# Scores of the first attention over all 128 rows of TensorE, with the queries doubled by on-chip transfers

## What is computed

```python
def diff_attention_mixer(h, hc, w_in, w_out, lam_p, subln_g, lam_init, cos, sin, with_ctx_out):
    # h: 256 tokens, hc: 256 context tokens; 8 heads, each with two query and two key vectors of 64 features
    q, k, v, z = project(h)
    qc, kc, vc, zc = project(hc)
    q, k = apply_rope(q, cos, sin), apply_rope(k, cos, sin)
    k_all, v_all = concat([k, kc]), concat([v, vc])
    def diff(qq, kk, vv, gate):
        o1 = sweep_attention(qq[..., 0, :], kk[..., 0, :], vv)     # softmax(q k / 8) v
        o2 = sweep_attention(qq[..., 1, :], kk[..., 1, :], vv)
        o = rms_norm(o1 - lam * o2, subln_g) * (1.0 - lam_init)
        return (o.reshape(B, L, 1024) * silu(gate)) @ w_out
    y = diff(q, k_all, v_all, z)          # tokens look at 512 keys
    yc = diff(qc, kc, vc, zc)             # the context looks at its own 256 keys
```

## Time and profile before

| | |
|---|---|
| median of 3 runs | 783.16 us |
| profiled execution, first to last instruction | 781.2 us |
| PE busy | 771.8 us, 99% |
| VectorE (DVE) busy | 550.9 us, 71% |
| ScalarE (ACT) busy | 395.9 us, 51% |
| chunks 1 to 5 of in0 | about 62 to 179.5 us |
| first attention, iterations 0 to 31 | 179.5 to 285 us |
| DMA in 193 to 278 us | 1% of the 16 engines, 1 GB/s |
| granted TensorE clock | 1.00 in every slice |

### The profile page before, as it was taken

How to read it: one execution, slowest core, us unless ns; L and a number is a source line. 1 busy time by engine, 2 the same in 40 slices (tenths; PEclk the granted TensorE clock), 3 DMA queues, 4 the chain that set the end, 5 groups by cost and what they waited for, 6 DMA issues and landing times.

```text
span 781.2 us, 10963 instructions
## 1 busy us (share of the span) xinstructions
PE 771.8 (99%) x4001; PEld 616.0 (79%) x4001; DVE 550.9 (71%) x988; ACT 395.9 (51%) x752; POOL 41.6 (5%) x54
## 2 busy tenths in 40 slices
PE   8999999999999999999999999999999999999998
PEld 5668777887777888867788888788788888888886
DVE  3356999797768868599767666998968554565553
ACT  4462323327788765475656656725444443443441
POOL 0020000000001010112100002200010000000000
PEclk9999999999999999999999999999999999999999
DMA  9995663344000075339222045963225745665621
GB/s 324 356 367 194 216 215 121 112 146 163 1 1 1 1 277 207 101 121 351 74 92 100 5 154 171 377 223 108 87 67 196 264 167 162 196 212 185 200 69 55
DMA packets 75576, 125.76 MB, mean 161 GB/s; under 512 B 2842, under 2 KB 36972, under 8 KB 75396
## 3 DMA queue, kind: packets, MB, share of 16 engines
q1 hardware_dynamic: 74576, 123.00, 45.8%
q10 hardware_dynamic: 532, 1.21, 0.5%
q0 software_dynamic: 416, 0.85, 0.4%
HBM read 123.99 MB, written 1.06 MB: 160 GB/s over the span
## 4 chain that ended last, share of the span: by engine, by line
PE 90%; DVE 3%; ACT 3%; DMA 1%; issue 1%; SPq 0%; POOL 0%; ACTq 0%; DVEq 0%
PE psum L869 18%; PE psum L871 17%; PE psum L870 16%; PE psum L858 4%; PE psum L859 4%; PE psum L860 4%; PE psum L1052 3%; PE psum L1077 3%; PE psum L977 3%; PE psum L1373 3%; PE psum L1371 3%; PE psum L1372 3%; PE psum L891 2%; PE psum L1150 2%; DMA raw<-in_a_w_in 1%
## 5 line engine op out<-in xcount | busy, mean ns | idle before, releaser
L870 PE MATMUL psum<-w_lo,act_hi 128*128 128x512 f32 (+1 forms) x624 | 242.0, 388 | 0.0
L869 PE MATMUL psum<-w_hi,act_hi 128*128 128x512 f32 (+1 forms) x584 | 237.5, 407 | 2.2 <-DVE act_lo L2173 2.0
L871 PE MATMUL psum<-w_hi,act_lo 128*128 128x512 f32 (+1 forms) x584 | 226.9, 389 | 0.0
L1992 DVE TENSOR_TENSOR w_lo<-raw,w_hi 128x2048 fp32r<-128x2048 f32 (+1 forms) x68 | 153.2, 2260 | 62.6 <-ACT w_hi L1410 62.5
L1410 ACT ACTIVATE w_hi<-raw 128x2048 fp32r<-128x2048 f32 (+1 forms) x72 | 136.2, 1895 | 70.6 <-PE psum L871 31.1
L869 PEld LDWEIGHTS psum<-w_hi,act_hi 128*128 128x128 f32 x584 | 109.6, 188 | 38.6 <-issue 14.4
L870 PEld LDWEIGHTS psum<-w_lo,act_hi 128*128 128x128 f32 x624 | 117.5, 188 | 20.5 <-issue 0.5
L871 PEld LDWEIGHTS psum<-w_hi,act_lo 128*128 128x128 f32 x584 | 109.6, 188 | 23.5
L1961 POOL TENSOR_TENSOR rstd<-ms,half_neg 128x1 f32<-128x1 f32 (+3 forms) x38 | 35.7, 940 | 523.3 <-DVE ms L2033 523.3
L858 PE MATMUL psum<-act_hi,w_hi 128*128 128x512 f32 x128 | 50.8, 397 | 0.0
L859 PE MATMUL psum<-act_lo,w_hi 128*128 128x512 f32 x128 | 49.9, 390 | 0.0
(11 more groups left out here) (292 smaller groups left out, 1133.5 us busy)
## 6 DMA issues: line engine op xcount, KB each, us to landing
raw<-in_a_w_in SPq DMA_DIRECT2D x16, 1024.0 KB, 8.7
raw<-in_ada_w SPq DMA_DIRECT2D x14, 1024.0 KB, 5.3
raw<-in_w_out SPq DMA_DIRECT2D x12, 1024.0 KB, 5.3
raw<-in_w_gate SPq DMA_DIRECT2D x22, 512.0 KB, 4.1
raw<-in_w_up SPq DMA_DIRECT2D x22, 512.0 KB, 5.1
raw<-in_w_down SPq DMA_DIRECT2D x11, 1024.0 KB, 4.9
raw<-in_b_w_in SPq DMA_DIRECT2D x10, 1024.0 KB, 7.5
raw<-in_w_in SPq DMA_DIRECT2D x10, 1024.0 KB, 5.9
```

The costliest lines, as they stand in the source:

```text
L869: pe.matmul(oh, x_hi, hi, start=(k == 0), stop=False)
L870: pe.matmul(o[:, 0:n], x_hi, lo, start=False, stop=False)
L871: mm = pe.matmul(oh, x_lo, hi, start=False, stop=(k == KT - 1))
L1992: ins = dve.tensor_tensor(rest, weights, hi.bitcast(F32), ALU.subtract)
```

## The change

- The keys' units (n = 8 to 15) are laid out anew. `round_k` holds for s = 0 the rounded features on rows 0 to 63 and their rests on rows 64 to 127; `rest_k` holds for s = 1 the rests on rows 0 to 63 and the rounded features on rows 64 to 127. Each rounding and each rest of a key unit becomes two instructions on 64 partitions. Queries stay as they are.
- The queries' rounded parts and rests are copied by SP into `doubled`, once on each half of the partitions, for both s: 8 transfers of 64 partitions by two rows of 512 B for a pair of steps (64 KB each), 128 transfers for the 16 pairs. `doubled` has room for four steps and lies in the slot of `w_lo` of a new entry ("doubled") in the list of loads, behind in0 6, so one of the six buffers stays empty from there to the load out0 (1,1).
- Pairs 0 and 1 are copied at that entry, which waits for the release of `ada0g` (1,0) (`s_sumused` >= 1). Pairs 2 and 3 stand ahead of the load out0 (0,0), pairs 4 to 8 ahead of out0 (0,1), pairs 9 to 15 ahead of out0 (1,0). From pair 2 on each waits until the scores of step 2\*pair-3 are there.
- A step's scores are four matmuls over 128 rows: for each s, the doubled rounded queries and then the doubled rests against the key tile. They also compute the product of the two rests. PE waits on `s_doubled` for the pair ahead of each step.

```diff
@@ loads_plan
+        elif c == 6:
+            plan.append(("doubled", 0, 0))
+DOUBLED_BEFORE = {("out0", 0, 0): range(2, 4), ("out0", 0, 1): range(4, 9), ("out0", 1, 0): range(9, 16)}
@@ emptied
+            if stage == "doubled":
+                b, at = place[("s0", NT * HEADS - 1, 1)]
+                emptied[n] = (full[b], at + 1)
@@
+        doubled = w_lo[:, doubled_at, :].rearrange("p (s r i n) -> p s r i n", s=2, r=4, i=2)
@@ SyncE
+            def doubled_queries(pair):
+                t, h = STEPS0[2 * pair]
+                if pair == 0:
+                    sp.wait_ge(s_rest0, HEADS)
+                elif pair >= 2:
+                    b, at = place[("s0", 2 * pair - 3, 1)]
+                    sp.wait_ge(full[b], at + 1)
+                r = slice(2 * (pair % 2), 2 * (pair % 2) + 2)
+                tokens = round_q[:, h, :].rearrange("p (s t n) -> p s t n", s=2, t=XT)[:, :, t, :].bitcast(F32)
+                rests = rest_q[:, 2 * pair:2 * pair + 2, :].bitcast(F32)
+                for s, own in enumerate((LOW, HIGH)):
+                    for half in (LOW, HIGH):
+                        sp.dma_start(doubled[half, s, r, 0, :].bitcast(F32), tokens[own]).then_inc(s_doubled[pair % 2], 16)
+                        sp.dma_start(doubled[half, s, r, 1, :].bitcast(F32), rests[own]).then_inc(s_doubled[pair % 2], 16)
...
+                if loads[n][0] == "doubled":
+                    sp.wait_ge(*emptied[n - RAW])
+                    for pair in range(2):
+                        doubled_queries(pair)
+                    continue
+                for pair in DOUBLED_BEFORE.get(loads[n], ()):
+                    doubled_queries(pair)
@@ features0
             if n < HEADS:
-                return round_q[:, h, tokens].rearrange("p (t n) -> p t n", t=XT), rest_steps[:, :, h, s, :], 0.125
-            return [buf[:, h, tokens].rearrange("p (t n) -> p t n", t=XT) for buf in (round_k, rest_k)] + [1.0]
+                return [(slice(0, P), by_tile(round_q[:, h, tokens]), rest_steps[:, :, h, s, :])], 0.125
+            return [(own, by_tile(buf[own, h, tokens]), by_tile(buf[other, h, tokens]))
+                    for buf, own, other in ((round_k, LOW, HIGH), (rest_k, HIGH, LOW))], 1.0
@@ scores0
-                o = [begin(("s0", p, s)) for s in range(2)]
-                for i in range(3):
-                    for s in range(2):
-                        rows = slice(64 * s, 64 * s + 64)
-                        q = rest_q[rows, p, :] if i == 2 else round_q[rows, h, tile_cols(t)]
-                        k = (rest_k if i == 1 else round_k)[rows, h, keys]
-                        mm = pe.matmul(o[s][:, 0:n], q, k, start=(i == 0), stop=(i == 2))
-                        if i == 2:
-                            mm.then_inc(bank_full(("s0", p, s)), 1)
+                pe.wait_ge(s_doubled[p // 2 % 2], 128 * (p // 4 + 1))
+                for s in range(2):
+                    o = begin(("s0", p, s))
+                    k = (round_k, rest_k)[s][:, h, keys]
+                    for i in range(2):
+                        mm = pe.matmul(o[:, 0:n], doubled[:, s, p % 4, i, :], k, start=(i == 0), stop=(i == 1))
+                    mm.then_inc(bank_full(("s0", p, s)), 1)
@@ ScalarE, round_x (round_context alike)
-                seq.note(act.activation(dst, src, ACTF.Copy, scale=scale).then_inc(s_qx, 1), s_qx)
+                for own, dst, _ in parts:
+                    ins = act.activation(dst, by_tile(rotated0(n)[own]), ACTF.Copy, scale=scale)
+                seq.note(ins.then_inc(s_qx, 1), s_qx)
@@ VectorE, rest_x (the context's rest in rotate0 alike)
+                for own, hi, lo in parts:
+                    ins = dve.scalar_tensor_tensor(out=lo, in0=by_tile(rotated0(n)[own]), scalar=scale, in1=hi.bitcast(F32),
+                                                   op0=ALU.mult, op1=ALU.subtract)
+                seq.note(ins.then_inc(s_rest0, 1), s_rest0)
```

## The result

The changed kernel takes 790.26 us (median of four runs, 789.36 to 791.97), the kernel before 783.12 in the same session: a ratio of 1.0092 (95% interval 1.0079 to 1.0105), 7.1 us slower. Forecast were 781.0 and a range of 777.0 to 785.5. The profiled execution is the longest of the four, a span of 789.9 us against 781.2; the others' spans are 787.4 to 788.5. Places are therefore compared by their starts, the size by the medians.

A forecast was written before the change was run, and what follows sets the result against it. PE, busy 99% of the span, was taken to bound the kernel. Start +3.4, pair 9 +0.3 and steps -5.9 gave -2.2 us on a span of 781.2, so 779.0, or 781.0 as median; range 777.0 to 785.5.

The forecast's parts named there:

- The passes: PE's scores: four full-height passes save 0.17 us in a heavy step, 0.30 in a light one, 0.46 a pair.
- passes only: Rival: edges of half-height passes aren't won back, each step is a pass longer: 791.7 us, chance 0.06.
- Where that gain counts: Attention steps: 14 pairs at 0.46 us, less 0.5 beside weight splits, gain 5.9 us, between 4.2 and 6.7.
- Key units on VectorE: Ahead of the attention: 16 more instructions make VectorE 3.6 us late; PE stalls 3.4 us at the first transposes.
- The clock: In the costlier-start rival, chance 0.2: PE's stand might drop the clock from 2.4 to 1.2 GHz; no row prices it.
- The first transfers: Pair 0's copies land at 175.6; PE waits 2.9 us at step 0's scores, inside the 3.4 us start loss.
- The other transfers: Later pairs need 5.5 us of about 9.5 available, so each is hidden; pair 9 costs 0.3 us.
- The sum: Whole kernel: +3.4 start, +0.3 pair 9, -5.9 steps, together -2.2 us.

The follow-up runs named there:

- The passes alone: Kernel before with four full-height score passes a step on undoubled queries, old key layout, no transfers: 781.10 us, ratio 0.9971.
- The later gates: Changed kernel with copies started earlier and GpSimd making token rests, plus tanh and its product moved behind probabilities' move and next combination: 782.17 us, 783.12 without this edit.
- key halves alone: Changed kernel's half-height key units with the old six score passes, no doubled queries and no transfers: 789.41 us against 783.13, ratio 1.0077.
- early copies: Changed kernel with the ring entry for the query copies ahead of in0 6 and pairs copied earlier: 787.74 us, ratio 1.0058.
- the split inside: Kernel with early copies, VectorE splitting the second half of in0's chunk 5 inside its key unit of (4,2): 789.50 us, ratio 1.0076.
- the split of in0 (6,0) moved: Kernel with early copies, VectorE's split of in0 (6,0) moved ahead of the key unit of (5,0): 792.51 us, ratio 1.0120.
- keys whole: Changed kernel with key units in whole instructions as before; transfers, ring entry and four passes as changed: 783.14 us, ratio 1.0003.

## Why the forecast was wrong, step by step

**The passes: the size per step was right.** Heavy: transposes to L1096 0.36 us (186.21, 186.57), as forecast, and to L914 1.37 (187.58), where the forecast's terms give 0.36 + 0.31 + 3 x 0.23 = 1.36. Light: 0.14 and 0.70 (189.15, 189.29, 189.85), forecast 0.67. The rival "passes only" is out: the edges are won back, and two iterations can take 6.16 us.

**Where that gain counts: wrong.** I took 0.46 us for each of 14 pairs and 0.5 off for places beside the splits. The passes alone gave 2.0 us. I had checked VectorE against the shorter step (0.13 us of room) and not ScalarE, whose move of the probabilities made PE wait 0.2 us in one place already. In every other pair it became the later one. The later gates show that the place of the tanh and its product is a part of it, 0.95 us of the 3.9 missed; the rest of these is argued from the waits, not tested.

**Key units on VectorE: right mechanism, too small.** Forecast 3.6 us late, measured 6.06 at the zeroing. Of these 0.65 stood at 109.45, ahead of the first key unit; from that split to the zeroing it is 62.98 us against 57.57 before, 5.4 us more (62.98, 62.99 and 62.87 in the profiles of key halves alone, early copies and the split inside). Three terms were mis-sized. The added instructions were taken at 0.36 us, but all four of a unit went to 0.43 to 0.46, so a unit grew by 1.09 and not 0.72: from the fifth unit's start to the end of the eighth 4.0 us (a wait of 0.33 absorbed), and 0.43 for the last half, 4.4 in all where I had 3.2 less 0.33. The wait of 2.81 us did not take up all that came before it; the fifth unit starts 1.20 late, with 0.33 allowed, and 0.65 of it is not the key units'. ScalarE's answer costs 0.42 instead of 0.33. The sum is 1.20 + 4.0 + 0.42 + 0.43 = 6.05. The split of in0 (5,1) ended 4.1 us late and not 2.2, so TensorE stalled 2.56 and not 1.2, on top of 0.49 that it was late already.

The Trainium skill, "VectorE: DVE Perf Modes", section on the trn2 errata, says that the latency of SBUF is exposed between instructions; it does not speak of half the partitions. The half-height rests, 0.42 us long and 0.43 or more apart, agree. The full-height one that reads SBUF alone, 0.41 us long at 142.69, is followed by the next instruction at 143.02, after 0.33: that doesn't agree, and here the measurement decides.

**The clock: named, not priced.** I left its fall out of the sum as no row had a price. Rows now have one: 1.6 us behind the first wait (from 163.35 to 166.33 seven starts at 0.43 instead of 0.23, and the ends), 1.3 behind the second (195.81 to the next heavy transposes at 203.26 is 7.45 us, a pair later 203.61 to 209.79 is 6.18; of this 0.86 is eight values matmuls in 1.91 us instead of 1.05). The first is covered but for the 0.6 us at step 0, by the run with the stall taken away; the second lies in the attention, where nothing covers it in this execution. In the median the two weigh less than that: the clock's fall differs between executions of one kernel. Of the four of the changed kernel one has a mean granted clock of 1.000 and takes 790.28 us, as long as the median; the profiled one, with 0.996, takes 791.97. With early copies the two executions at 1.000 and 0.999 take 787.72 and 787.44 us, the two at 0.998 take 787.75 and 788.10: where the first fall is covered it hardly shows in the time.

**The first transfers: mis-sized.** Issues were taken at 0.43 us from whole loads; a copy of this shape takes 0.61, one every 0.65. Landing was right (2.1 against 2.1). So pair 0 landed at about 179.2 and its scores waited till 179.26. As forecast this lies beside VectorE's late start and adds little to it, a part of the 0.6 us above: the scores are 6.6 us late, the first maximum 6.2 (181.47 against 175.29), the first transposes 6.7.

**The other transfers: wrong.** I gave each pair three iterations, took 2 us to landing and called the DMA engines idle. Left out was the order at the start: the queue issues pairs 0 and 1 one behind the other, then two loads of 1 MB (together 1.17 us), and only then pair 2. Its last issue is at 190.11, and the scores of step 4 would have started at 193.7. With 2.1 us to landing it would still have been in time, at 192.2; behind the two loads it took 5.6 us and landed at 195.7. The scores waited 2.06 us for it, and the second fall of the clock follows. This is why step 4 is 3.5 us later than step 0, and why early copies give 2.5 us back. The later pairs are hidden, pair 9 but for 0.3 us, as forecast.

**The sum put right**, by the runs: key halves +6.3 where I had +3.4, passes -2.0 where I had -5.9, copies +2.0 where I had +0.3 (my sum was -2.2). The measured 7.1 leaves 0.8, which is within the noise of the runs. PE's own 0.6 us at step 0 and the clock's second fall may be in it; the execution at a clock of 1.000, no faster than the median, speaks against the clock. It stays open.

## What to carry to other kernels

An engine that is busy 99% hides what the others do, until it is made faster: before counting a gain per step, take the same time out of the step for every engine that feeds it, ScalarE's moves out of PSUM too, and look which comes last. Here cutting an operation by partitions more than doubled its cost (1.77 us for 0.68); put the extra work where the chain ahead of the next stage doesn't pass, or on an idle engine. For a burst of small copies, count the issue time on the queue from its first to its last, in the order in which the queue holds them, and take the time to landing from copies that stand behind loads as large, not from a copy alone.

## What the runs showed of the hardware that I had not expected

- Half-height rests on VectorE (64x256) are listed with 0.42 us, like full-height ones, but start 0.43 apart and not 0.34. They also write to other partitions than they read, and which of the two it is stays open.
- A copy of 64 KB on the chip, 64 partitions with two rows each, holds SyncE's queue for 0.61 us, and 2.0 to 2.1 us pass from its issue to its landing. Issued behind two loads of 1 MB each it took 5.2 to 7.4 us. The Trainium skill, "DMA: Bandwidth & Descriptors", section on the anatomy of one DMA, gives about 2.0 us as the fixed cost of a DMA issued by GpSimd; these are issued by SyncE, and those with no load ahead of them come to the same.
- After a wait of 2.56 us with TensorE at full work on both sides, its clock fell to 1.2 GHz for about 3 us; after one of 2.42 (early copies, 0.57 from 163 to 167) as well; after one of 2.48 at the same place (the split of in0 (6,0) moved) it stayed at 1.00. Waits of like length near this one either gave 1.6 us of lower clock more or none. Behind a wait of 1.76 us in the attention (keys whole) the clock stayed at 1.00, behind 2.06, 3.96 and 5.32 it fell.
- GpSimd's subtraction of 64x256 takes 0.73 to 1.12 us, mostly 0.74, but 2.85 where it starts beside a split on VectorE (2.29 us long): it ends 0.6 us after VectorE's. Once the split took 2.82 us instead of 2.29, with GpSimd's first subtraction beside it. The two engines' instructions stood in each other's way here.
